# Gate and up of the small experts through one joined operand, and a bias of distances stored in reverse

## What is computed

```python
# layer 0: a bias by the distance of query and key is added to every softmax logit
la = einsum('bqhd,bqkd->bhqk', qa, ka) * scale + moveaxis(bias_a[rel_bucket(t[None, :, None] - sel_a)], -1, 1)

# layer 1: two of eight experts for each token
top_v, top_i = lax.top_k(h @ w_router, TOP_K)
for e in range(N_EXPERTS):
    y = y + gates[..., e:e + 1] * swiglu(h, w_gate[e], w_up[e], w_down[e])   # 1024 -> 3584 -> 1024
# swiglu(h, wg, wu, wd) = (silu(h @ wg) * (h @ wu)) @ wd
```

## Time and profile before

| | us |
|---|---|
| median of 3 runs | 1389.4 |
| lowest and highest of them | 1388.17, 1390.34 |
| the profiled execution | 1391.95 |
| its span, first to last instruction | 1390.1 |
| seven whole experts (places 1 to 7) in it | 582.6 to 1378.6 |
| PE busy, DVE busy, ACT busy in the span | 1363.8, 1102.2, 924.2 |

### The profile page before, as it was taken

How to read it: one execution, slowest core, us unless ns; L and a number is a source line. 1 busy time by engine, 2 the same in 40 slices (tenths; PEclk the granted TensorE clock), 3 DMA queues, 4 the chain that set the end, 5 groups by cost and what they waited for, 6 DMA issues and landing times.

```text
span 1390.1 us, 16748 instructions
## 1 busy us (share of the span) xinstructions
PE 1363.8 (98%) x6662; PEld 1062.6 (76%) x6662; DVE 1102.2 (79%) x858; ACT 924.2 (66%) x723; POOL 50.9 (4%) x51
## 2 busy tenths in 40 slices
PE   8998999999999999999999999999999999999997
PEld 7886788887988888766788866688886668887664
DVE  4686554446455999899999888898898999988898
ACT  3566434343544877777877777778777787777774
POOL 1000000000000000000000000000000000002000
PEclk9999999999999999999999999999999999999999
DMA  9654555554633799999999999999999999999994
GB/s 310 209 168 146 164 188 183 182 182 156 222 122 121 281 387 394 363 372 415 400 403 399 395 379 378 412 391 416 400 362 396 383 407 398 404 400 374 412 405 155
DMA packets 136643, 439.14 MB, mean 316 GB/s; under 512 B 11520, under 2 KB 28912, under 8 KB 120816
## 3 DMA queue, kind: packets, MB, share of 16 engines
q1 hardware_dynamic: 130688, 424.24, 80.9%
q0 software_dynamic: 3392, 12.07, 2.5%
q10 hardware_dynamic: 2480, 1.69, 0.4%
HBM read 432.20 MB, written 5.78 MB: 315 GB/s over the span
## 4 chain that ended last, share of the span: by engine, by line
PE 87%; DVE 8%; ACT 2%; DMA 1%; issue 1%; ACTq 0%; DVEq 0%
PE ps L1892 25%; PE ps L1894 25%; PE ps L1893 25%; DVE lo L1213 3%; PE ps L2377 3%; PE ps L2378 3%; PE ps L2440 2%; DMA work<-bias_by_distance 1%; DVE work L1239 1%; DMA bias_by_distance<-diag_sb 0%; ACT hi L789 0%; PE ps L2188 0%; PE ps L1984 0%; DMA x<-in_x_dram 0%; PE ps L2348 0%
## 5 line engine op out<-in xcount | busy, mean ns | idle before, releaser
L1213 DVE TENSOR_TENSOR lo<-raw,hi 128x2048 fp32r<-128x2048 f32 (+1 forms) x403 | 903.7, 2282 | 102.5 <-ACT hi L789 101.4
L789 ACT ACTIVATE hi<-raw 128x2048 fp32r<-128x2048 f32 (+1 forms) x403 | 768.9, 1915 | 240.9 <-PE ps L1894 186.7
L1892 PE MATMUL ps<-hi,xT_hi 128*128 128x512 f32 (+2 forms) x1200 | 471.0, 393 | 3.2 <-DVE lo L1213 1.8
L1894 PE MATMUL ps<-hi,xT_lo 128*128 128x512 f32 (+2 forms) x1200 | 466.1, 388 | 0.0
L1893 PE MATMUL ps<-lo,xT_hi 128*128 128x512 f32 (+2 forms) x1200 | 465.9, 388 | 0.0
L1892 PEld LDWEIGHTS ps<-hi,xT_hi 128*128 128x128 f32 (+1 forms) x1200 | 202.1, 168 | 75.0 <-DVE lo L1213 2.6
L1894 PEld LDWEIGHTS ps<-hi,xT_lo 128*128 128x128 f32 (+1 forms) x1200 | 201.8, 168 | 71.4
L1893 PEld LDWEIGHTS ps<-lo,xT_hi 128*128 128x128 f32 (+1 forms) x1200 | 202.0, 168 | 67.5
L1892 PE MATMUL ps<-hi,hT_hi 128*128 128x512 f32 x296 | 116.1, 392 | 0.0
L1894 PE MATMUL ps<-hi,hT_lo 128*128 128x512 f32 x296 | 115.3, 390 | 0.0
L1893 PE MATMUL ps<-lo,hT_hi 128*128 128x512 f32 x296 | 115.2, 389 | 0.0
(11 more groups left out here) (316 smaller groups left out, 941.8 us busy)
## 6 DMA issues: line engine op xcount, KB each, us to landing
raw<-in_od_w_gate_dram SPq DMA_DIRECT2D x112, 1024.0 KB, 8.6
raw<-in_od_w_up_dram SPq DMA_DIRECT2D x112, 1024.0 KB, 9.0
raw<-in_od_w_down_dram SPq DMA_DIRECT2D x112, 1024.0 KB, 8.5
raw<-in_od_w_qkv_dram SPq DMA_DIRECT2D x12, 1024.0 KB, 5.3
raw<-in_ev_w_gate_dram SPq DMA_DIRECT2D x11, 1024.0 KB, 5.1
raw<-in_ev_w_up_dram SPq DMA_DIRECT2D x11, 1024.0 KB, 5.2
raw<-in_ev_w_down_dram SPq DMA_DIRECT2D x11, 1024.0 KB, 5.3
raw<-in_ev_w_in_dram SPq DMA_DIRECT2D x4, 1024.0 KB, 11.1
```

What stands on the lines that cost most here:

```text
L789: act.activation(unit(hi, n), unit(raw, n), ACT.Copy).then_inc(hi_ready, 1)
L1213: dve.tensor_tensor(unit(lo, n), unit(raw, n), unit(hi, n).bitcast(F32), ALU.subtract)\
L1892: pe.matmul(out, s_hi, m_hi, start=start, stop=False, skip_group_check=True)
L1894: return pe.matmul(out, s_lo, m_hi, start=False, stop=stop, skip_group_check=True)
```

## The change

It has two parts.

**The bias.** The one-hot rows that make the row by distance are reversed (`bucket_rows`), so that the shifted load from HBM has its partitions in the right order and runs backward along j. POOL loads it straight into `bias_kT`, masks it there, and `key_bias` hands DVE a view with a step of -1. `flip`, its products and the copies are gone.

**Gate and up of the small experts.** `gathered_low` writes the low part of the token rows into columns 64 to 127 of `xg_hi`, beside the high part. `columns` then does two products a bank with 128 columns. The rows 64 to 127 of the PSUM banks hold what belongs to the low part; they must be added to rows 0 to 63 before the silu and the multiply. ACT copies them to `work` (`keep_gate_low`, `keep_up_low`), and PE adds them to the rows above by one product a bank with a piece of the identity, in full float32 (`fold_gate`, `fold_up`). Silu waits for `gate_folded`, multiply for `up_folded`. The orders of PE, ACT and DVE in a small expert are written out anew.

```diff
-    return rows
+    return np.ascontiguousarray(rows[:, ::-1])
...
-            return bias_kT[:, heads, P * (1 - t):P * (1 - t) + keys(b)]
+            return bias_kT[:, heads, P * (1 + t) - keys(b):P * (1 + t)][:, :, ::-1]
...
-            pool.dma_start(hankel, bass.AP(tensor=diag_d.tensor, offset=diag_d.offset,
-                                           ap=[[1, P], [SEQ + P, CH], [1, SEQ]])).then_inc(hankel_loaded, 16)
-
-            pool.wait_ge(bias_copied, 4)
+            pool.dma_start(bias_kT[:], bass.AP(tensor=diag_d.tensor, offset=diag_d.offset + 1,
+                                               ap=[[1, P], [SEQ + P, CH], [1, SEQ]])).then_inc(bias_loaded, 16)
+
+            pool.wait_ge(bias_loaded, 16)
...
-            for a in range(4):
-                act.wait_ge(bias_flipped, a + 1)
-                act.activation(bias_kT[:, 2 * a:2 * a + 2, :], ps[:, 4 + a, :].rearrange("p (h s) -> p h s", h=2),
-                               ACT.Copy).then_inc(bias_copied, 1)
             splits_to(5)
...
+            def keep_gate_low(e, c):
+
+                w = MOE_CHUNKS[c][1]
+                act.wait_ge(units_used, first_of(e) + UP_AT[c])
+                act.wait_ge(g_h_done, NCH * e + c)
+                act.activation(work[HALF:P, 0, 0:w], ps[HALF:P, 4:4 + w // W, :].rearrange("p a n -> p (a n)"),
+                               ACT.Copy).then_inc(gate_low_kept, 1)
...
+                    if e in SMALL:
+                        used(UP_AT[0])
+                        keep_gate_low(e, 0)
+                        used(UP_AT[0] + 1)
+                        silu(e, 0)
+                        used(GATE_AT[1])
+                        keep_up_low(e, 0)
+                        used(UP_AT[1])
+                        keep_gate_low(e, 1)
+                        g_hT_high(e, 0)
+                        used(UP_AT[1] + 1)
+                        silu(e, 1)
+                        used(DOWN_AT[0])
+                        keep_up_low(e, 1)
...
+                    low = xg_hi[:, dst, HALF:P] if e in SMALL else xg_lo[:, dst, :]
...
-                dve.wait_ge(units_used, first_of(e) + UP_AT[c] + KD * w // UNIT)
+                if e in SMALL:
+                    dve.wait_ge(up_folded, small_chunks(e, c) + 1)
...
-            pe.wait_ge(hankel_loaded, 16)
-            pe.wait_ge(flip_ready, 2)
             pe.wait_ge(diag_copied, 1)
             pe.wait_ge(pos_copied, 1)
-            for a in range(4):
-                for h in range(2):
-                    ins = pe.matmul(ps[:, 4 + a, SEQ * h:SEQ * h + SEQ], flip[:], hankel[:, 2 * a + h, :],
-                                    start=True, stop=True)
-                ins.then_inc(bias_flipped, 1)
             project_T(2, 4, 2, parts=(1,))
...
+                        if e in SMALL:
+                            ins = both(ps[:, bank + m, :], xg_hi[:, k, :], wh[:, kk, cols], wl[:, kk, cols], k == 0,
+                                       k == KD - 1)
+                            continue
...
+                    if q == 0 and e in SMALL:
+                        fold_gate(e, c)
...
+            def fold_gate(e, c):
+
+                pe.wait_ge(gate_low_kept, small_chunks(e, c) + 1)
+                for m in range(MOE_CHUNKS[c][1] // W):
+                    ins = pe.matmul(ps[0:HALF, 4 + m, :], ident[HALF:P, HALF:P], work[HALF:P, 0, W * m:W * m + W],
+                                    start=False, stop=True, skip_group_check=True)
+                ins.then_inc(gate_folded, 1)
...
+                    if e in SMALL:
+                        fold_up(e, 0)
+                        gate(e, 1, 2, 3)
+                        g_transpose_h(e, 0, 0)
+                        up(e, 1, 0, 1, 2, 3)
+                        pe.wait_ge(y_copied, e)
+                        down(e, 0, 0, 1)
+                        fold_up(e, 1)
```

More of the change, by code:

```diff
@@ L641, in stores_before, with small_chunks @@
             return 16 * (e + len([i for i in SMALL if i < e]))
+        def small_chunks(e, c):
+            return NCH * len([i for i in SMALL if i < e]) + c
         def rows_of(e):
@@ L1087, in silu, with keep_up_low @@
                     .then_inc(g_silu_done, 1)
+            def keep_gate_low(e, c):
+                w = MOE_CHUNKS[c][1]
+                act.wait_ge(units_used, first_of(e) + UP_AT[c])
+                act.wait_ge(g_h_done, NCH * e + c)
+                act.activation(work[HALF:P, 0, 0:w], ps[HALF:P, 4:4 + w // W, :].rearrange("p a n -> p (a n)"),
+                               ACT.Copy).then_inc(gate_low_kept, 1)
+            def keep_up_low(e, c):
+                w = MOE_CHUNKS[c][1]
+                act.wait_ge(units_used, first_of(e) + UP_AT[c] + KD * w // UNIT)
+                act.wait_ge(g_hT_done, NSUB * e)
+                act.activation(work[HALF:P, 1, 0:w], ps[HALF:P, 2:2 + w // W, :].rearrange("p a n -> p (a n)"),
+                               ACT.Copy).then_inc(up_low_kept, 1)
             def g_hT_high(e, s):
@@ L1766, in _ @@
                         used(0)
+                    if e in SMALL:
+                        used(GATE_AT[1] + 2)
+                        multiply(e, 0)
+                        used(UP_AT[1])
+                        g_hT_low(e, 0)
+                        if e == 1:
+                            slot_numbers()
+                        used(GATE_AT[2])
+                        multiply(e, 1)
+                        if e + 1 < NE:
+                            make_place(e + 1)
+                        used(GATE_AT[2] + 2)
+                        g_hT_low(e, 1)
+                        used(UP_AT[2])
+                        g_hT_low(e, 2)
+                        if e + 1 < NE:
+                            pick(e + 1)
+                        used(DOWN_AT[1] + 2)
+                        multiply(e, 2)
+                        if e == NE - 1:
+                            add_result(0)
+                            used(GATE_AT[3])
+                            add_result(1)
+                        used(GATE_AT[3] + 2)
+                        g_hT_low(e, 3)
+                        if e == NE - 1:
+                            used(GATE_AT[3] + 3)
+                            add_result(2)
+                        used(UP_AT[3])
+                        g_hT_low(e, 4)
+                        if e == NE - 1:
+                            used(UP_AT[3] + 2)
+                            add_result(3)
+                        used(DOWN_AT[2] + 1)
+                        multiply(e, 3)
+                        used(DOWN_AT[2] + 3)
+                        g_hT_low(e, 5)
+                        used(DOWN_AT[3])
+                        if e + 1 < NE:
+                            gathered_low(e + 1)
+                        g_hT_low(e, 6)
+                        continue
                     used(GATE_AT[1])
@@ L2441, in g_transpose_h, with fold_up @@
                 ins.then_inc(g_hT_done, 1)
+            def fold_gate(e, c):
[4 more added lines that the diff above has]
+                ins.then_inc(gate_folded, 1)
+            def fold_up(e, c):
+                pe.wait_ge(up_low_kept, small_chunks(e, c) + 1)
+                for m in range(MOE_CHUNKS[c][1] // W):
+                    ins = pe.matmul(ps[0:HALF, 2 + m, :], ident[HALF:P, HALF:P], work[HALF:P, 1, W * m:W * m + W],
+                                    start=False, stop=True, skip_group_check=True)
+                ins.then_inc(up_folded, 1)
             def transpose_place(e):
@@ L2469, in _ @@
                     gate(e, 1, 0, 1)
+                    if e in SMALL:
+                        fold_up(e, 0)
[5 more added lines that the diff above has]
+                        fold_up(e, 1)
+                        if e == NE - 1:
+                            transpose_place(e)
+                        gate(e, 2, 0, 1)
+                        g_transpose_h(e, 1, 1)
+                        gate(e, 2, 2, 3)
+                        g_transpose_h(e, 2, 1)
+                        if e + 1 < NE:
+                            pick_rows(e + 1)
+                        up(e, 2, 0, 1, 2, 3)
+                        down(e, 1, 0, 1)
+                        fold_up(e, 2)
+                        down(e, 1, 2, 3)
+                        gate(e, 3, 0, 1)
+                        g_transpose_h(e, 3, 2)
+                        gate(e, 3, 2, 3)
+                        g_transpose_h(e, 4, 2)
+                        up(e, 3, 0, 1, 2, 3)
+                        down(e, 2, 0)
+                        fold_up(e, 3)
+                        down(e, 2, 1, 2)
+                        g_transpose_h(e, 5, 3)
+                        down(e, 2, 3)
+                        if e + 1 < NE:
+                            gather(e + 1)
+                        g_transpose_h(e, 6, 3)
+                        down(e, 3, 0, 1, 2, 3)
+                        continue
                     g_transpose_h(e, 0, 0)
```

64 lines of the change are left out of this document (45 added, 19 removed).

## The result

| | before | after |
|---|---|---|
| median, us | 1389.66 (4 runs) | 1379.79 (4 runs) |
| lowest and highest | 1388.17, 1390.34 | 1378.45, 1381.05 |
| ratio, 95% interval | | 0.9933 [0.9921, 0.9945] |
| the profiled execution, its span | 1391.95, 1390.1 | 1379.38, 1377.6 |

The kernel is faster by 9.9 us, 0.7%. 24.6 us were forecast. The direction is right and the time lies in the range, but the gain is 40% of the forecast one.

What follows compares the result with a forecast made beforehand. PE was taken as the bound, with DVE, ACT and data close behind. Terms of -6.6 (head), -4.5, -5.5, -5.5 and -2.5 (experts 1, 3, 5, 7) summed to -24.6, median 1364.8 us, range 1350 to 1383.

Steps and rivals of the forecast that it cites:

- What bounds before: All experts: PE is the bound at 0.23 us a product, 109.6 us a small expert and 119.1 a large one.
- The head: Before the projection: without the flip its products start at 33.6 for 40.22, a gain of 6.6 us.
- The backward read and POOL's load: Bias: DVE's read with step -1 costs 0 (far bound +4.3 us); POOL's load and mask are hidden, over 25 us to spare.
- Rival D: Bias on DVE: the backward read is slow, 1.7 times as long, +4.3 us, 1369 us in all; chance 0.07.
- PE's own part: Small experts: 25.8 us of products less, 12.6 of fold products more; PE alone from 109.6 to 96.4 us.
- The data: A large and a small expert: 90.1 MB at 406 to 408 GB/s, so a pair loses at most 6.9 to 7.9 us.
- The folds at 0: Small experts: PE's waits for ACT's copies cost 0, covered by some 0.7 us where data have landed.
- rival C: Small experts: late data delay ACT's copies, 2.3 us at each of 32 folds, 73.6 us, 1404 in all; chance 0.06.
- C's break-even: Small experts: waits turn the change slower from 1.86 us a fold, the gross gain of 59.4 us over 32 folds.
- Expert 7: Last small expert: only its first 31 us can gain, up to 2.9 us; 2.5 us taken.
- The clock (rival E): Small experts: 3.4 us at half clock once in each if folds leave gaps, 6.8 us, 1371.6 in all; chance 0.05.
- Large experts: Large experts: nothing changes, PE stays their bound at 119.1 us if DVE and data keep up; 0.

Runs made afterwards that it cites:

- experiment 2: The changed kernel without the copies of the low rows and the products that add them: 1366.39 us, 0.9836 of the kernel before.
- experiments 6 and 7: Half of each weight unit of experts 1 to 7 transferred, in the changed kernel (1349.14 us) and in the changed kernel without folds and copies (1343.17).
- experiment 9: The changed kernel with ACT's copy of gate's low rows one split later: 1397.11 us, 1.0067 of the kernel before.
- Experiments 4 and 10: Expert 7 back in its old form, in the changed kernel (1377.90 us) and in the one with both copies ahead (1371.49).
- experiment 8: The changed kernel with ACT's copy of gate's low rows, and in chunk 3 of up's too, ahead of the split: 1373.18 us, 0.9900 of before.

## Why the prediction was right in part and wrong in size

**What bounds before: right.** PE at 0.23 us a product was the bound of small and large experts; half of the data changed nothing in either.

**The head: mechanism right, size off in the medians.** 6.6 us forecast, 6.8 in the traces, 4.4 in the medians. The sum was made against one profiled execution that was 2.5 us above the median, and was then carried to the median whole. Part of what it was above, a second stretch at half clock, lay in the head, and a stretch came back behind the head when the flip's was gone.

**The backward read and POOL's load: right**, 0. Rival D did not occur.

**PE's own part: right.** A fold product was put at 0.9 us; in expert 5 the next product starts 1.00 us after a fold of one bank and 1.86 after a fold of two. PE alone was forecast at 96.4; the small expert without late data takes 98.6. ACT's busy time is 93.1 (92.6 forecast), and DVE's idle time 8.4 us (106.60 - 98.19), where half of 12.1 had been taken.

**The data: right, as long as nothing else is late.** Pairs were forecast to lose at most 6.9 to 7.9 us by their bytes, and without folds experts 4 and 5 lose 7.1. I took 5.5 for experts 3 and 5 and 4.5 for expert 1, and got 4.0, 3.0 and 3.2; without folds they give 6.4, 7.4 and 6.0, less 0.3 to 0.5 in each large one.

**The folds at 0: the step that failed.** The prediction had the chain in full (fold behind the copy, copy behind the split of the unit three ahead, split behind the data), and covered the copy by 0.7 us "where data have landed". It then put the small experts at the rate at which data have *not* landed, and still took the cover. The two terms can't stand together: taking 13 us of products off a kernel whose transfers have 7 to give makes the splits wait for their data (10.0 us in expert 5, 2.9 before), and that is the condition of rival C. The size is in experiment 2: without folds and copies the kernel takes 1366.39, 1.6 us above the forecast of 1364.8, and with them 1379.79. So 13.4 of the 15.0 us that the forecast was low are what folds and copies cost; 6.0 of them are left when data are early (experiments 6 and 7). That the rest is so small is luck in part: the small experts gave more than forecast, and the head and expert 7 less.

The waits were 16.2 us in 9 places against C's 73.6 in 32: PE, 7.4 us behind DVE's splits at the start of expert 5 and 3.5 at its end, could take most late copies. C's break-even of 1.86 us at each of 32 folds, 59.4 us in all, was itself far too high, since the data never let the gross gain out: in experiment 9, 28.0 us of waits at 16 folds, with the clock lost behind them, made the kernel slower than before.

**Expert 7: wrong in sign**, 2.5 us of gain forecast, 4.5 lost. Its window was read for its first 31 us, in which data had room. But two other limits stood beside PE's 109.9 us. One is DVE: before, it has no idle time from 1339 to the end of its last split at 1376.42, and PE takes that unit 0.06 us later:

```profile
1374.15 2.27 DVE L1213 TENSOR_TENSOR lo<-raw,hi 128x2048 fp32r<-128x2048 f32 x1
...
1376.48 0.50 PE L2377 MATMUL ps<-hi,hT_lo 128*128 128x512 f32 x1
```

The other is the data. They were not the bound before (half of them left 109.9), but with all of them the joined form gets no shorter. Without folds the last unit lands and is split 97.7 us into the expert (39.5 MB, so 404 GB/s), and what follows it takes 13.3 more:

```profile
1341.32 1.92 ACT L788 ACTIVATE hi<-raw 128x2048 fp32r<-128x2048 f32 x1 [0.16 <-DMA raw<-in_od_w_down_dram]
```

That is 111.0, 1.1 above the old form; with half of the data and no folds it is 101.9. So, with the full data, nothing taken off PE shortened expert 7. The other 3.4 us are what the folds cost: two waits of 2.4 and 2.2 us ahead of them, with half clock behind. Experiments 4 and 10 give the loss back, and with both copies ahead (experiment 8) the joined form takes 110.7.

**The clock (rival E)** was to cost one stretch in each small expert, 6.8 us in all, at 5%. The stretches came: one in experts 1 and 3, two in 5, three in 7, one of them twice as long. The Trainium skill ("TensorE: Matmul & The Clock Gate", section "HAM oscillation — how this bites in real kernels") warns of waits within a loop of products that bring the clock down for the products behind them. The trace agrees: PE had waited 0.94 to 2.48 us ahead of the folds before the stretches in experts 1, 3 and 5. But a wait of 0.94 us with a slow stretch behind it (at 1072) and one of 1.47 without (at 1047) stand in the same expert. What the stretches cost by themselves isn't shown; where PE waits for data anyway, it may have been little.

**Large experts: right**, 119.1 to the tenth.

## What to carry over

When an engine is relieved, work out for each engine and for the transfers how much they allow, and then price every new wait in the state that the tightest of them leaves, not in the state that the trace of before shows: an in-order engine that splits data as they land makes everything behind that split late by as much as the data are. A small operation on which the bound engine waits belongs ahead of the data-bound one on its queue, as long as data are late. And a part of the program whose data end with the engine's work (here the last expert) gains nothing from fewer products, and pays for what comes with them.

## What was not expected of the hardware

- One core's transfers held 408 to 410 GB/s over whole experts of 102 to 107 us, as high as in the short stretches before, and a pair with a large expert reached the time of its bytes at that rate (221.6 us).
- Runs of the kernels with both copies ahead scatter more than others: 1369.8 to 1377.2 and 1367.9 to 1375.4 in experiments 8 and 10, against 1387.4 to 1390.1 before. That data are the bound is not enough to explain it: without folds, where ACT's splits wait longest for data (19.2 us in expert 5), the four runs lie within 1365.7 to 1367.9. The cause is open.
- POOL's mask over the bias took 2.67 us after and 1.94 before, with the same number of elements; after, DVE was busy beside it. No run tells whether that or the pattern is the cause; it was hidden.
